# Output projections with weights in blocks of 3, 3, 1 and 1 column chunks, and six output chunks begun in the last head units

## What is computed

```python
def trunk(x):                                  # cut to what matters here
    h = rms_norm(x, attn_norm[0]); x = x + sliding_sink_attention(h) @ a_w_out
    x = x + conv_ffn(rms_norm(x, ffn_norm[0]))
    h = rms_norm(x, attn_norm[1]); x = x + differential_attention(h) @ b_w_out
    x = x + conv_ffn(rms_norm(x, ffn_norm[1]))
    return rms_norm(x, final_norm)
```

## Time and profile before

| | us |
|---|---|
| median of 3 runs | 1174.99 (1174.76 to 1175.63) |
| profiled execution | 1174.54 |
| its span, from first to last instruction | 1172.8 |
| PE busy | 1140.1 (97%) |
| DVE busy | 688.9 (59%) |
| ACT busy | 462.2 (39%) |
| mean granted TensorE clock | 0.994 of full speed |

### The profile page before, as it was taken

One profiled execution on the slowest core, in us unless ns is written; L12 is line 12 of the kernel. 1 busy time (PEld: TensorE's weight loads), 2 busy tenths in 40 slices (PEclk: granted clock), 3 DMA queues, 4 the chain that ended last, 5 costly groups with the idle time before them and its releaser, 6 DMA issues.

```text
span 1172.8 us, 15982 instructions
## 1 busy us (share of the span) xinstructions
PE 1140.1 (97%) x5752; PEld 966.2 (82%) x5752; DVE 688.9 (59%) x1153; ACT 462.2 (39%) x939; POOL 19.0 (2%) x36
## 2 busy tenths in 40 slices
PE   7999899999999999998999999999999999999997
PEld 6998688888888878887999988778888888888886
DVE  5588765565565553337577777855556556553334
ACT  6577653122122222336455556554212212222324
POOL 4100000000000000000000000000000000000000
PEclk8999999999999999999999999999999999999999
DMA  7211223323323222325112311214332332213222
GB/s 225 72 37 37 73 88 92 96 84 107 105 74 107 72 72 94 102 89 162 55 54 69 94 36 36 72 40 122 108 92 86 107 103 76 89 54 105 92 91 106
DMA packets 146603, 101.94 MB, mean 87 GB/s; under 512 B 12073, under 2 KB 139270, under 8 KB 146566
## 3 DMA queue, kind: packets, MB, share of 16 engines
q1 hardware_dynamic: 146566, 101.45, 28.1%
HBM read 99.34 MB, written 2.10 MB: 86 GB/s over the span
## 4 chain that ended last, share of the span: by engine, by line
PE 87%; DVE 7%; ACT 4%; issue 1%; DMA 1%; SPq 0%; DVEq 0%; ACTq 0%
PE ps L529 22%; PE ps L531 22%; PE ps L530 21%; PE ps L594 15%; PE ps L608 2%; PE ps L746 2%; ACT prob L1091 1%; DVE w_lo L1354 1%; DVE h_lo L1383 1%; PE ps L772 1%; PE ps L818 1%; DVE ot_lo L1563 1%; ACT w_hi L1014 1%; ACT prob L1101 1%; DVE den L1441 0%
## 5 line engine op out<-in xcount | busy, mean ns | idle before, releaser
L1014 ACT ACTIVATE w_hi<-raw 128x512 fp32r<-128x512 f32 (+2 forms) x212 | 192.5, 940 | 302.6 <-PE ps L531 299.7
L529 PE MATMUL ps<-h_hi,w_lo 128*128 128x512 f32 x704 | 274.7, 390 | 0.0
L531 PE MATMUL ps<-h_hi,w_hi 128*128 128x512 f32 x704 | 273.9, 389 | 0.0
L530 PE MATMUL ps<-h_lo,w_hi 128*128 128x512 f32 x704 | 273.9, 389 | 0.0
L1354 DVE TENSOR_TENSOR w_lo<-raw,w_hi 128x512 fp32r<-128x512 f32 (+2 forms) x204 | 215.6, 1082 | 6.2 <-ACT w_hi L1014 6.2
L530 PEld LDWEIGHTS ps<-h_lo,w_hi 128*128 128x128 f32 x704 | 132.1, 188 | 27.9 <-issue 0.5
L529 PEld LDWEIGHTS ps<-h_hi,w_lo 128*128 128x128 f32 x704 | 132.1, 188 | 27.7 <-issue 0.5
L531 PEld LDWEIGHTS ps<-h_hi,w_hi 128*128 128x128 f32 x704 | 132.1, 188 | 27.6
L594 PE MATMUL ps<-w_hi,h_lo 128*128 128x384 f32 x384 | 133.4, 347 | 8.6 <-DVE w_lo L1354 4.5
L594 PE MATMUL ps<-w_hi,h_hi 128*128 128x384 f32 x384 | 133.2, 347 | 0.0
L594 PE MATMUL ps<-w_lo,h_hi 128*128 128x384 f32 x384 | 132.5, 345 | 0.0
(11 more groups left out here) (188 smaller groups left out, 1583.2 us busy)
## 6 DMA issues: line engine op xcount, KB each, us to landing
raw<-in_ffn_w_up SPq DMA_DIRECT2D x88, 512.0 KB, 4.5
raw<-in_ffn_w_down SPq DMA_DIRECT2D x44, 512.0 KB, 3.3
raw<-in_b_w_in SPq DMA_DIRECT2D x24, 512.0 KB, 4.9
raw<-in_a_w_out SPq DMA_DIRECT2D x4, 1024.0 KB, 4.9
raw<-in_b_w_out SPq DMA_DIRECT2D x4, 1024.0 KB, 4.7
raw<-in_a_w_in SPq DMA_DIRECT2D x3, 1024.0 KB, 5.8
x_tok<-in_x SPq DMA_DIRECT2D x4, 512.0 KB, 4.8
out<-x_tok SPq DMA_DIRECT2D x8, 256.0 KB, 2.0
```

Source lines behind the costliest of these rows:

```text
L529: pe.matmul(out_, a_lo, b_hi, start=start, stop=False)
L530: pe.matmul(out_, a_hi, b_lo, start=False, stop=False)
L531: return pe.matmul(out_, a_hi, b_hi, start=False, stop=stop)
L1014: act.activation(w_hi[:, s, at], raw[:, s, at], ACT.Copy).then_inc(hi_done, 1)
```

## The change

The out weights come in blocks of 3, 3, 1 and 1 chunks (`OUT_BLOCKS`): 3072, 3072, 1024 and 1024 columns of a slot, each again in four parts. Every output chunk has a bank of its own, given free by the waits of the new `bank_free`. Chunks 0 to 5 are begun in the last units, with new numbers in `n`. The mean square of the last head goes to bank 5 (`LAST_MS`) so that chunk 2 can hold TB. In `after_out` blocks 2 and 3 and up block 0 are converted whole, at chunks 0, 3 and 6 on ACT and 2, 5 and 6 on DVE. The first up pair waits for fewer chunks of `x_ready` (2 and 5 in place of 6 and 8).

```diff
@@ -42,16 +42,17 @@
...
 UA, UB = 4, 8
-OB, ODC = 4, 2
+OUT_BLOCKS = ((0, 3), (3, 3), (6, 1), (7, 1))
+OB = len(OUT_BLOCKS)
 PHASES = {}
...
 for _name, _n, _cols, _dmas, _cut in (
-        ("attnA", UA, KC * UW, 3, 4), ("outA", OB, KC * ODC * P, 1, 4),
+        ("attnA", UA, KC * UW, 3, 4), ("outA", OB, None, 1, 4),
         ("up0", FB, KC * 2 * P, 2, 1), ("down0", FB, D, 1, 2),
-        ("attnB", UB, KC * UW, 3, 4), ("outB", OB, KC * ODC * P, 1, 4),
+        ("attnB", UB, KC * UW, 3, 4), ("outB", OB, None, 1, 4),
         ("up1", FB, KC * 2 * P, 2, 1), ("down1", FB, D, 1, 2)):
@@ -192,9 +193,11 @@
...
         PJ, TB, OBK = (0, 1), 6, 7
-        OUT_BANKS = ((0, 1, TB, 3), (0, 1, 2, 3))
+        OUT_BANKS = ((0, 1, TB, 3, 2, 5, 4, OBK), (0, 1, TB, 3, 2, 4, 5, OBK))
         OUT_AHEAD = (6, 7)
+        LAST_MS = 5
         def s_bank(t):
@@ -339,8 +342,14 @@
             return PHASES[ph][4] + 16 * PHASES[ph][3] * (turn + 1)
-        def cols(ph):
-            return PHASES[ph][2]
+        def cols(ph, i=0):
+            return KC * P * OUT_BLOCKS[i][1] if ph[:3] == "out" else PHASES[ph][2]
+        def out_block(dc):
+            for b, (dc0, n) in enumerate(OUT_BLOCKS):
+                if dc0 <= dc < dc0 + n:
+                    return b, dc - dc0
         def parts(ph):
@@ -379,7 +388,7 @@
...
             elif ph[:3] == "out":
-                eng.wait_ge(oproj_done, i * ODC + (KC * l + ODC))
+                eng.wait_ge(oproj_done, KC * l + sum(OUT_BLOCKS[i]))
             elif ph[:2] == "up":
@@ -423,8 +432,9 @@
...
                     wv = w[0].rearrange("(k p) n -> p k n", p=P)
-                    rv = raw[:, s, 0:cols(ph)].rearrange("p (k n) -> p k n", k=KC)
-                    sp.dma_start(rv, wv[:, :, bass.ds(i * ODC * P, ODC * P)])\
+                    dc0, n = OUT_BLOCKS[i]
+                    rv = raw[:, s, 0:cols(ph, i)].rearrange("p (k n) -> p k n", k=KC)
+                    sp.dma_start(rv, wv[:, :, bass.ds(dc0 * P, n * P)])\
                       .then_inc(raw_landed[s], 16)
@@ -696,12 +706,12 @@
...
                 else:
-                    ahead = chain(out_ahead(0, (2,), range(6)), out_ahead(0, (0, 1), range(4, 6)),
-                                  out_ahead(0, (3,), range(6)))
+                    ahead = chain(out_ahead(0, (2,), range(4)), out_ahead(0, (0, 1, 2), range(4, 6)),
+                                  *(out_ahead(0, (dc,), range(6)) for dc in (3, 4, 5)))
                 slabs = chain(projection("A", u + 1, (u + 1) % 2, (2, 3)) if more else (), ahead)
                 n = (4, 3, 5, 2, 2, 2, 1, 1, 4) if u + 2 < UA else (4, 3, 5, 1, 1, 1, 1, 1, 3) if more \
-                    else (3, 0, 3, 0, 3, 0, 1, 0, 4)
+                    else (4, 1, 4, 1, 4, 0, 2, 0, 4)
                 probs_a(u, 0)
@@ -782,14 +792,15 @@
...
                 elif more:
-                    ahead = out_ahead(1, (0, 1), range(3))
+                    ahead = out_ahead(1, (0, 1), range(4))
                 else:
-                    ahead = chain(out_ahead(1, (0, 1), range(3, 7)), out_ahead(1, (3,), range(7)),
-                                  out_ahead(1, (2,), range(7)))
+                    ahead = chain(out_ahead(1, (0, 1), range(4, 6)), out_ahead(1, (2,), range(6)),
+                                  out_ahead(1, (0, 1, 2), range(6, 7)),
+                                  *(out_ahead(1, (dc,), range(7)) for dc in (3, 4, 5)))
                 slabs = chain(projection("B", u + 1, 1 - s, (2, 3)) if more else (), ahead)
-                n = (4, 4, 4, 2, 2, 1, 3, 3, 1) if more2 else (4, 4, 4, 1, 1, 1, 2, 1, 0) if more else \
-                    (4, 2, 2, 0, 4, 0, 0, 4, 1)
+                n = (4, 4, 4, 2, 2, 1, 3, 3, 1) if more2 else (4, 4, 4, 1, 2, 2, 2, 1, 0) if more else \
+                    (4, 2, 4, 0, 6, 0, 0, 5, 2)
                 probs_b(u, 0)
@@ -815,37 +826,52 @@
...
                 pe.wait_ge(osq_done, u + 1)
-                pe.matmul(ps[:, TB, :], ones_d[:, :], osq[:, :], start=True, stop=True)\
+                pe.matmul(ps[:, TB if more else LAST_MS, :], ones_d[:, :], osq[:, :], start=True, stop=True)\
                   .then_inc(oms_done, 1)
...
             def out_products(l, dc, chunks):
-                ph, s = ("outA", "outB")[l], dc // ODC % 2
-                wh = w_hi[:, s, 0:cols(ph)].rearrange("p (k n) -> p k n", k=KC)
-                wl = w_lo[:, s, 0:cols(ph)].rearrange("p (k n) -> p k n", k=KC)
-                c = slice(dc % ODC * P, (dc % ODC + 1) * P)
+                ph, (b, e) = ("outA", "outB")[l], out_block(dc)
+                wh = w_hi[:, b % 2, 0:cols(ph, b)].rearrange("p (k n) -> p k n", k=KC)
+                wl = w_lo[:, b % 2, 0:cols(ph, b)].rearrange("p (k n) -> p k n", k=KC)
+                c = slice(e * P, (e + 1) * P)
                 for kc in chunks:
-                    ins = hi_lo(ps[:, OUT_BANKS[l][dc % 4], :], wh[:, kc, c], wl[:, kc, c],
+                    ins = hi_lo(ps[:, OUT_BANKS[l][dc], :], wh[:, kc, c], wl[:, kc, c],
                                 ot_hi[:, kc, :], ot_lo[:, kc, :], start=(kc == 0), stop=(kc == KC - 1))
...
                     ins.then_inc(oproj_done, 1)
+            def bank_free(l, dc):
+                last = ("AB"[l], (UA, UB)[l] - 1)
+                if dc < 2:
+                    pe.wait_ge(vlo_done, tile_no(*last, NT - 1))
+                elif dc == 2 and l == 1:
+                    pe.wait_ge(oln_done, UB - 1)
+                elif dc == 3:
+                    pe.wait_ge(exp_done, tile_no(*last, 2))
+                elif dc == 4:
+                    pe.wait_ge(plo_done, tile_no(*last, 2))
+                elif dc == 5 and l == 0:
+                    pe.wait_ge(exp_done, tile_no(*last, 3))
+                elif dc == (6 if l == 0 else 5):
+                    pe.wait_ge(plo_done, tile_no(*last, 3))
+                elif dc == 6:
+                    pe.wait_ge(oln_done, UB)
+                elif dc == 7 and l == 1:
+                    pe.wait_ge(otmp_done, UB)
             def out_ahead(l, dcs, chunks):
...
                     for dc in dcs:
-                        pe.wait_ge(lo_done, part_done(ph, dc // ODC, kc * parts(ph) // KC))
+                        pe.wait_ge(lo_done, part_done(ph, out_block(dc)[0], kc * parts(ph) // KC))
                         if kc == 0:
-                            last = ("AB"[l], (UA, UB)[l] - 1)
-                            if dc < 2:
-                                pe.wait_ge(vlo_done, tile_no(*last, NT - 1))
-                            elif dc == 2 and l == 1 or dc == 3 and l == 0:
-                                pe.wait_ge(plo_done, tile_no(*last, 2))
-                            elif dc == 3:
-                                pe.wait_ge(exp_done, tile_no(*last, 2))
+                            bank_free(l, dc)
                         pe.wait_ge(olo_done, NT * (kc // 2 + 1) if l == 0 else NT * UA + kc + 1)
@@ -853,17 +879,16 @@
...
                 pe.wait_ge(olo_done, NT * UA + UB * l)
-                norm = NORM["F0"] if l == 0 else NORM["F1"]
                 for dc in range(KC):
-                    if dc >= 4:
-                        pe.wait_ge(x_ready, KC * norm + dc - 3)
-                    ahead = OUT_AHEAD[l] if dc < 4 else 0
+                    ahead = OUT_AHEAD[l] if dc < 6 else 0
+                    if not ahead:
+                        bank_free(l, dc)
                     ph = ("outA", "outB")[l]
...
                         if rows:
-                            pe.wait_ge(lo_done, part_done(ph, dc // ODC, c))
+                            pe.wait_ge(lo_done, part_done(ph, out_block(dc)[0], c))
                             out_products(l, dc, rows)
@@ -883,7 +908,7 @@
...
                     if is_first:
-                        pe.wait_ge(x_ready, KC * norm + (6 if s == 0 else KC))
+                        pe.wait_ge(x_ready, KC * norm + (2 if s == 0 else 5))
                     order = [(g, kc) for g in range(2) for kc in range(KC)]
@@ -1004,7 +1029,7 @@
...
                     return
-                n = cols(ph) // parts(ph)
+                n = (cols(ph, 2 * turn + s) if ph[:3] == "out" else cols(ph)) // parts(ph)
                 at = slice(c * n, (c + 1) * n)
@@ -1201,13 +1226,12 @@
...
                 ph, norm = ("outA", "outB")[l], NORM["F0"] if l == 0 else NORM["F1"]
-                for b in range(OB):
-                    for e in range(ODC):
-                        dc = ODC * b + e
-                        gained(norm, dc, vecT[:, l, R_FFN + dc:R_FFN + dc + 1])
-                        square(norm, dc)
-                        for c in range(2):
-                            high_after(ph, b, 2 * e + c)
+                for dc in range(KC):
+                    gained(norm, dc, vecT[:, l, R_FFN + dc:R_FFN + dc + 1])
+                    for b in {0: (0,), 3: (1,), 6: (2,)}.get(dc, ()):
+                        high_whole(ph, b)
+                    square(norm, dc)
+                high_whole(ph, 3)
```

(12 more changed lines are left out.)

## The result

| | kernel before | changed kernel |
|---|---|---|
| median, 7 runs each | 1175.12 (1174.76 to 1176.52) | 1179.31 (1177.43 to 1181.00) |
| ratio, with its 95% interval | | 1.0035 (1.0023 to 1.0047) |
| profiled execution, its span | 1174.54, 1172.8 | 1177.80, 1176.0 |
| PE busy | 1140.1 | 1138.7 |
| mean granted clock of that execution | 0.994 | 0.996 |

The change costs 0.35%, 4.2 us. The forecast was 1177.2, with a range of 1172.8 to 1180.0: the direction and the range held, the size was half of what was measured. All times are in us.

What follows compares the result with a forecast made beforehand. TensorE (PE), busy 97% of the span, was taken as the bound, so only its idle time could move. Layer A +1.3 and B +0.9 us added 2.2 to 1174.99, giving 1177.2, range 1172.8 to 1180.

Steps and rivals of the forecast that it cites:

- Part 1: Last head units: more output slabs begun ahead fill PE's holes; -2.9 us in A, -0.8 and -2.3 in B.
- Part 2: Head units: 768-column parts of blocks 0 and 1 delay DVE and ACT; +1.6 us in A, +0.85 in B.
- Part 3: Behind the output projections: weight conversions come late and PE waits; +2.5 to 2.6 us in A, +3.1 in B.
- the old hole's 1.6: Layer B's projection: the present wait for block 2's w_lo, 1.35 us plus 0.25, set against the new waits.
- The sum: Whole kernel: all terms added per layer, +1.3 us in A and +0.9 in B.
- The sum takes no clock loss: Whole kernel: small holes of 0.37 to 1.35 us leave the granted clock at 1.00, so nothing is added.
- Rival 4: Burst behind the projections: granted clock falls, 0.75 to 1.5 us in each layer, giving 1179.5; chance 0.03.
- The first: Behind the projections: ACT and DVE keep up, no late conversions, giving 1169.8; chance 0.15.
- The second: Last head units: added slabs push the chain instead of filling holes, +3 us, giving 1180.2; chance 0.14.
- the third: Last head units: bank or weight waits keep six outputs from beginning early, giving about 1176; chance 0.05.

Runs made afterwards that it cites:

- all: Changed kernel with the edits of early, unitsA and unitsB together: 1165.5 us, ratio 0.9915 to the kernel before.
- all_nofill: The kernel all, but with the slabs ahead and numbers between steps of the kernel before: 1172.8 us, ratio 0.9976.
- early: Changed kernel with the weight conversions behind the projections moved forward in ACT's and DVE's order: 1171.6 us, ratio 0.9971.
- unitsA: Changed kernel with block 1's conversion spread over the last two head units, layer A only: 1175.0 us, ratio 0.9994.
- ctl: The changed kernel run again without any edit: 1179.2 us, ratio 1.0028 to the kernel before.
- nofill: Changed kernel with only as many slabs ahead as the kernel before (24 and 28), blocks and banks as changed: 1178.8 us, ratio 1.0034.
- unitsB: Changed kernel with block 1's conversion spread over the last two head units, layer B only: 1178.2 us, ratio 1.0019.
- before_hole: Kernel before with two unused DVE additions behind block 1's w_lo in A's unit 2, enlarging the hole there: 1177.7 us, ratio 1.0017.
- units: Changed kernel with block 1's conversion spread over the last two head units in both layers: 1175.0 us, ratio 0.9994.

## Why the prediction was right or wrong

- **Part 1, -2.9 and -3.1.** Measured -3.4 in A and -3.1 in B by `all` against `all_nofill`. Right in mechanism and place (no hole left in A's unit 3, 0.17 in B's unit 7); A's term was 0.5 too small. That the waits for the four added banks cost nothing held as well: in the changed kernel no out matmul waits for an exp or an Ln. The bank that was waited for is chunk 0's, an old one (0.55, next point).
- **Part 2, +1.6 and +0.85.** A's term is right, +1.63 from S to values(3) of unit 2; its place is half right. The hole there grew by 1.07, from 1.11 to 2.18, and not to the 2.7 that the prediction named as a sign: that is the four parts of 0.27 ahead of low_p. The 0.55 for the three parts ahead of divide(2) came too, but 15 us earlier, as the new hole before the first output slab. The chain had no slack there. B's +0.85 is the 0.86 of ACT; the hole it makes grows from 0.24 to 1.10.
- **Part 3, holes of 1.8, 1.1 and 1.6 in B, 0.85 and 1.6 in A.** Measured 1.74, 0.98 and 1.30, and 0.84 and 1.36. Right in every place and in the engine that ends them; the last one of each layer 0.3 too large. The step of a part of 256 columns, which no row of before showed, was taken as 0.33 on DVE and 0.30 to 0.31 on ACT: four took 1.43 and 1.35, so the straight line held. The reason given, that DVE first finishes what stands ahead of `w_lo`, is what `early` takes away, and all the waits with it. As a whole the term was +2.5 to 2.6 in A, where `all` against `unitsA` gives 2.7. In B it was 4.7 without the old hole's 1.6, and `early` against the changed kernel gives 4.7.
- **The sum, +1.3 and +0.9.** +1.26 and +0.82, and within A +1.63 and -0.37 where the terms make +1.6 and -0.3. For the executions with the higher mean clock the forecast of 1177.2 meets 1177.3 to 1177.8.
- **"The sum takes no clock loss" is the step that failed.** The direction and the range held; the half of the size that is missing is this term, put at nothing. Nine of 14 executions have the lower mean clock, and their mean is 2.8 above that of the other five; this carries the median from 1177.5 to 1179.3. Where the loss lies is known for one of the nine, `ctl`'s profile: 2.55 behind the hole of part 2, 0.65 before it, 0.8 behind the 4.4 hole at M. `unitsA` shows that without part 2's hole the lower group is gone. The argument was that holes of 0.37 to 1.35 left the clock at 1.00, and that a hole of 4.5 did not. The sum itself said that part 2 would make a hole of 2.7, between these rows, and did not ask what the clock would do there. (The hole came out at 2.18, still between them.) Rival 4 named the clock, but looked at the burst behind the projection, where it stays at 1.00 (750 to 800 and 800 to 850 in the profile of every kernel here), and took 0.03 for it. The Trainium skill (TensorE: Matmul & The Clock Gate, A second HAM failure mode) speaks of frequent small pauses between groups of matmuls; the runs don't show that at the five small holes of the projections, and do show a fall behind one hole of 2.2. One execution in eleven (`ctl` at 119) has a fall behind two small holes, 0.53 and 0.62, which is nearer to what the Trainium skill describes there.
- **The chances.** Slower had 0.44, the same as within 0.2%, since 1177.2 lay on the border of 1177.3. A clock that could fall once per execution has no gain beside its loss, and would have moved the forecast over that border.
- **The rivals.** The first (conversions in time, 1169.8) did not happen, but it is what the order of `early` makes: 1171.6 with the holes of part 2 still in it. The second (added slabs push the chain) is refuted by `all_nofill`, where the slabs give all of part 1, and `nofill` fits that; the third is refuted by the trace, and the fourth by the clock of 1.00 behind both projections. That 1179.5, the time of rival 4, lies next to the measured 1179.3 is chance: its mechanism did not occur.

## What to carry to other kernels

A bank for each output lets PE run ahead, but it takes away the turns in which the in-order engines used to convert the next weights: ask for each conversion behind such a burst which instructions its engine finishes first, and move them, which here was worth 7.7 us by the medians and 6.3 by the traces, for no added work. Where a sum makes one hole larger than any that the trace shows at full clock, price it twice, once by its length and once by the clock that may fall behind it. And judge a filler together with the cure of what comes behind it: the same slabs were worth nothing that could be measured in the changed kernel (`nofill`) and 6.5 us with the conversions in order. Last, follow a delay along the whole chain that it enters: it can come out as a wait long before the one that was expected, as the 0.55 before the first slab did.

## What the runs showed of the hardware

- Behind the hole before values(3) of A's unit 2 the granted clock was below 1.00 in five of the six profiles with a hole there of 2.14 to 2.29 (`ctl`, `nofill`, `early`, `unitsB`, `before_hole`: 0.86 to 0.93 in 125 to 150; the changed kernel itself: 1.00), and 1.00 in the five with a hole of at most 1.2 or none (before, `units`, `unitsA`, `all`, `all_nofill`). It went to 0.50 and stayed there for 3 to 4 us, in `ctl` for almost 7, while PE worked with no hole above 0.4.
- It is not that place alone: `ctl` has 0.93 in 100 to 125 as well, where the holes are 0.5 to 0.7. Behind the 4.4 at M, which all kernels have, the clock falls to 0.50 in all eleven profiles: 530 to 560 shows 0.94 in seven and 0.89 in four. The four (`ctl`, `nofill`, `unitsB`, `before_hole`) are four of the five that also fell in A's unit 2. Why one execution has the fall, or the longer one, and the next has not stays open.
- What a fall costs is not fixed: from values(3) to U0 it is 2.55 in `ctl` (7 us at half clock), 1.5 in `unitsB` and 0.2 in `before_hole` (3 to 4 us at half clock in each), against the same stretch of the changed kernel or the kernel before at 1.00. In `before_hole` PE has further holes right behind it, which may take up the delay; no run tests that.
- The start of the same program, up to S, took between 47.1 and 48.9 in these profiles.
